# Delta rule: rows of decays put on all partitions by loads from memory, all sample states scaled on GpSimd during the input projection

## The reference

```python
g = -exp(a_log) * softplus(a_pre + dt_bias)          # log decay per token and head
gc = cumsum(g, within a chunk)
dmat = where(incl, exp(gc[:, None] - gc[None, :]), 0)
a_mat = strict lower part of (k * beta) k^T * dmat    # solved as (I + a_mat)^-1
qk = lower part of q k^T * dmat
q_dec, k_dec, g_last = q * exp(gc), k * exp(gc[last] - gc), exp(gc[last])
# chunk by chunk: v_new = u - w S ; o = q_dec S + qk v_new ; S = S g_last + k_dec^T v_new
```

## Time and profile before

| | |
|---|---|
| time before, median of 3 runs | 1590.81 us (1590.49 to 1592.78) |
| the profiled execution's own time | 1594.32 us |
| its span | 1592.6 us |
| busy: PE, DVE, ACT, POOL | 98%, 66%, 56%, 16% |
| granted PE clock and transfers, 98 to 104 us | 1.00, 176 GB/s |
| the same, 116 to 122 us | 1.00, 10 GB/s |
| the same, 128 to 134 us | 1.00, 0 GB/s |
| weight loads of 1 MB, median from issue to landing | 5.0 to 5.4 us for most, 8.3 for the delta rule's input weights |

### The profile page before, as it was taken

The page is one execution under the profiler, slowest core; times in us unless marked ns, Lnnn a source line. Parts: engine busy times, 40 slices in busy tenths (PEclk is TensorE's granted clock), DMA queues, the critical chain, the costliest instruction groups (busy, mean ns, idle before and its releaser), DMA issues.

```text
span 1592.6 us, 37769 instructions
## 1 busy us (share of the span) xinstructions
PE 1563.1 (98%) x16212; PEld 1481.5 (93%) x16212; DVE 1055.5 (66%) x1732; ACT 884.4 (56%) x1696; POOL 256.2 (16%) x328
## 2 busy tenths in 40 slices
PE   9999999999999999999999999999999999999997
PEld 7998799999997999999788888999999997999997
DVE  7965686755757877547793747776469837767643
ACT  6856656633645666434652546665358547566433
POOL 7105450000110200003003421100010035400000
PEclk9999999999999999999999999999999999999999
DMA  8941456565753665653635003665569512565550
GB/s 244 292 140 29 134 164 179 183 206 175 255 160 133 200 176 185 195 185 94 189 96 144 20 7 98 176 185 186 186 182 261 174 55 82 165 181 184 188 167 28
DMA packets 245529, 250.10 MB, mean 157 GB/s; under 512 B 16270, under 2 KB 239284, under 8 KB 245300
## 3 DMA queue, kind: packets, MB, share of 16 engines
q1 hardware_dynamic: 237204, 224.78, 46.3%
q0 software_dynamic: 8016, 22.86, 4.9%
q10 hardware_dynamic: 144, 0.05, 0.0%
HBM read 229.75 MB, written 18.32 MB: 156 GB/s over the span
## 4 chain that ended last, share of the span: by engine, by line
PE 92%; ACT 4%; DVE 3%; issue 1%; DMA 0%; SPq 0%; DVEq 0%
PE ps L844 88%; PE ps L848 4%; ACT vk L2053 1%; ACT tri L2053 1%; ACT acts L2053 1%; ACT st L2053 0%; DVE acts L2760 0%; ACT hn L2053 0%; DVE tri L2752 0%; DVE acts L2752 0%; DMA acts<-in_x_sample_dram 0%; ACT L2056 0%; PE ps L1796 0%; DVE st L2760 0%; DVE hn L2760 0%
## 5 line engine op out<-in xcount | busy, mean ns | idle before, releaser
L2752 DVE TENSOR_TENSOR w_mlp<-ring,w_mlp 128x1024 fp32r<-128x1024 f32 x256 | 311.7, 1224 | 119.9 <-ACT w_mlp L2053 113.9
L2053 ACT ACTIVATE w_mlp<-ring 128x1024 fp32r<-128x1024 f32 x256 | 269.4, 1054 | 208.2 <-PE ps L844 208.2
L844 PE MATMUL ps<-hn_split,w_mlp 128*128 128x264 f32 x3072 | 373.3, 284 | 0.0
L844 PE MATMUL ps<-h_split,w_mlp 128*128 128x264 f32 x3072 | 372.6, 283 | 0.0
L844 PEld LDWEIGHTS ps<-hn_split,w_mlp 128*128 128x128 f32 x3072 | 372.0, 188 | 0.3
L844 PEld LDWEIGHTS ps<-h_split,w_mlp 128*128 128x128 f32 x3072 | 371.6, 188 | 0.0
L2053 ACT ACTIVATE tri<-ps 128x264 f32<-128x264 f32 (+4 forms) x222 | 101.4, 463 | 181.2 <-PE ps L844 156.2
L844 PE MATMUL ps<-gdn_hi,w_gdn 128*128 128x264 f32 x896 | 165.8, 285 | 0.0
L844 PEld LDWEIGHTS ps<-gdn_hi,w_gdn 128*128 128x128 f32 x896 | 139.3, 188 | 0.9 <-issue 0.8
L844 PE MATMUL ps<-mixer_lo,w_gdn 128*128 128x264 f32 x448 | 126.9, 283 | 0.0
L2752 DVE TENSOR_TENSOR tri<-tri 128x264 f32<-128x264 f32 (+4 forms) x145 | 59.7, 413 | 101.3 <-ACT h_split L2053 100.6
(11 more groups left out here) (454 smaller groups left out, 2654.2 us busy)
## 6 DMA issues: line engine op xcount, KB each, us to landing
ring<-in_ffn_w_dram SPq DMA_DIRECT2D x128, 1024.0 KB, 5.4
ring<-in_gdn_w_in_dram SPq DMA_DIRECT2D x32, 1024.0 KB, 8.3
ring<-in_ml_w_in_dram SPq DMA_DIRECT2D x12, 1024.0 KB, 5.5
ring<-in_rw_w_rkv_dram SPq DMA_DIRECT2D x12, 1024.0 KB, 5.0
st<-in_state_gdn_S_dram POOLq DMA_DIRECT2D x2, 4096.0 KB, 22.4
ring<-in_gdn_w_out_dram SPq DMA_DIRECT2D x8, 1024.0 KB, 5.0
out_gdn_S_s_dram<-st SPq DMA_DIRECT2D x16, 512.0 KB, 6.8
st<-in_state_mlstm_C_dram POOLq DMA_DIRECT2D x1, 4096.0 KB, 20.5
```

The source lines that it names most:

```text
L844: return nc.tensor.matmul(out, lhsT, rhs, start=start, stop=stop)
L2053: return nc.scalar.activation(out, in_, f, bias=bias, scale=scale)
L2752: return nc.vector.tensor_tensor(out, in0, in1, op)
```

## The change

1. ACT, `gate_logs`: behind the logarithm it waits for DVE's `g_ok` and takes the exponential of the samples' 8x8 log decays (`eg_ev`). POOL puts it on a diagonal, PE multiplies it by ones in a new hook after u = 6 (`sample_decays`), and DVE copies the product to `E6[:, 5]` at n = 14.
2. POOL scales all eight heads of the sample states right behind that, during the projection. ACT's scaling is gone, and the outer products wait for no scaling.
3. The four `spread` calls and `spread_queries` are gone. After u = 13 PE makes one product of 16 rows and 256 columns. ACT copies it (log rows), takes its exponential and stores both in memory with five transfers from its own queue. POOL waits for them and issues three loads that repeat the rows: two of 64 partitions by 8 KB (into `AT6` and `QK6`), one of 128 partitions by 8 KB (into `QS`). DVE waits for all three before it adds `negC` to both matrices.
4. In `decay_exponents` five `ccol` products are left; POOL's two memsets now stand ahead of `rtx`. `statio` lies in another part of `acts`.

```diff
@@ PE
-                    for half in range(2):
-                        spread(0, 4 + half, half)
+                    b = 4
+                    pe.wait_ge(*last_read[b])
+                    mm(ps[b][0:2 * GH, 0:SEQ], selt[:, 0:2, :].rearrange("p a h -> p (a h)"), RG[:, 0:SEQ]).then_inc(row_mm, count.up(row_mm))
...
-                    for q in range(6):
+                    for n, q in enumerate((0, 1, 2, 3, 5)):
...
                 def query_exponents():
-                    for half in range(2):
-                        spread(4, 4 + half, half)
...
+                def sample_decays():
+                    pe.wait_ge(egd_ok, count.seen(egd_ok))
+                    b = 6
+                    pe.wait_ge(*last_read[b])
+                    mm(ps[b][:, 0:GH * NS], ones[0:GH, :], rows[0:GH, 1, 0:GH * NS]).then_inc(eg_mm, count.up(eg_mm))
...
-                fills = {(0, 0): sample_products, (0, 1): spread_queries, (1, 0): sample_outputs,
+                fills = {(0, 0): sample_products, (1, 0): sample_outputs,
@@ ACT, gate_logs
+                    ac.wait_ge(g_ok, count.seen(g_ok, 4 if j else 1))
+                    act(rows[0:GH, 1, SEQ:T], RG[0:GH, SEQ:T], ACT.Exp).then_inc(eg_ev, count.up(eg_ev))
@@ ACT, n == 27
+                        ac.wait_ge(row_mm, count.seen(row_mm))
+                        act(row_log, ps[4][0:2 * GH, 0:SEQ], ACT.Copy)
+                        act(row_exp, ps[4][0:2 * GH, 0:SEQ], ACT.Exp).then_inc(row_ev, count.up(row_ev))
+                        ac.wait_ge(row_ev, count.own(row_ev))
+                        for q in range(2):
+                            for g in range(2):
+                                at = q * GH + 4 * g
+                                ac.dma_start(exp_rows[j][g, q].rearrange("c h i -> h c i"),
+                                             rows[at:at + 4, 3, 0:SEQ].rearrange("h (c i) -> h c i", c=4)).then_inc(
+                                                 row_out, count.up(row_out, 16))
+                        ac.dma_start(query_rows[j], rows[0:GH, 4, 0:SEQ]).then_inc(row_out, count.up(row_out, 16))
...
-                    if n in (29, 30):
-                        ac.wait_ge(da_ok, count.seen(da_ok, 2))
-                        part = AT6 if n == 29 else QK6
-                        act(part, part, ACT.Exp).then_inc(dt_ok, count.up(dt_ok))
+                    if n == 30:
+                        for part in (AT6, QK6):
+                            ac.wait_ge(da_ok, count.seen(da_ok))
+                            act(part, part, ACT.Exp).then_inc(dt_ok, count.up(dt_ok))
@@ DVE
+                    if n == 14:
+                        dv.wait_ge(eg_mm, count.seen(eg_mm))
+                        copy(E6[:, 5], ps[6][:, 0:GH * NS]).then_inc(egs_ev, count.up(egs_ev))
...
-                exponents(QK6, 4, 0)
-                exponents(QK6, 5, 1)
+                dv.wait_ge(negc_ok, count.seen(negc_ok))
+                dv.wait_ge(spr_in, count.seen(spr_in, 48))
+                for part in (AT6, QK6):
+                    tt(part, part, negC, ALU.add).then_inc(da_ok, count.up(da_ok))
@@ POOL
+                for h in range(GH):
+                    s_ = sth[:, h]
+                    gp_.tensor_tensor(s_, s_, bc(E6[:, 5, h * NS:(h + 1) * NS], P, 2), ALU.mult).then_inc(
+                        st_sc, count.up(st_sc))
                 po.wait_ge(rt_ok, count.seen(rt_ok))
-                gp_.tensor_tensor(hs8(rtx), bc(RG[:, SEQ:T], GH, 1), bc(mh[:], NS, 2), ALU.mult).then_inc(rtx_ok, count.up(rtx_ok))
                 gp_.memset(statio, 0.0)
                 gp_.memset(vv, 0.0)
+                gp_.tensor_tensor(hs8(rtx), bc(RG[:, SEQ:T], GH, 1), bc(mh[:], NS, 2), ALU.mult).then_inc(rtx_ok, count.up(rtx_ok))
+                po.wait_ge(row_out, 80 * (j + 1))
+                for g, r in enumerate(halves):
+                    load(A(5).rearrange("p a b -> p (a b)")[r, 0:2 * D], bc(exp_rows[j][g].rearrange("s c h i -> (s c h i)"), HD, 0), spr_in)
+                load(QS.rearrange("p h t -> p (h t)"), bc(query_rows[j].rearrange("h t -> (h t)"), P, 0), spr_in)
```

More of the change, by code:

```diff
@@ L444, in hybrid_trunk @@
         ot_mm = oq_mm
-        qe_mm = rt_mm
         smp_mm = h_mm
         sp_mm = sw_mm
-        spread_mm = kk_mm
         ssq_ok = qs_ok
+        scan_ok = da_ok
+        row_mm = rt_mm
+        row_ev = rt_ok
+        egd_ok = qs_ok
+        qd_ok = st_sc
+        eg_mm = kk_mm
+        egs_ev = s_ok
         sums_mm = ct_mm
@@ L469, in hybrid_trunk @@
                     for i in range(2))
+        exp_rows = [nc.dram_tensor(f"exp_rows{n}", (2, 2, 4, 4, HD), F32, kind="Internal").ap() for n in range(2)]
+        query_rows = [nc.dram_tensor(f"query_rows{n}", (GH, SEQ), F32, kind="Internal").ap() for n in range(2)]
+        row_log, row_exp = rows[0:2 * GH, 3, 0:SEQ], rows[0:2 * GH, 4, 0:SEQ]
         QS = A(6).rearrange("p a b -> p (a b)")[:, 0:2 * D].rearrange("p (h t) -> p h t", h=GH)
-        statio = A(6).rearrange("p a b -> p (a b)")[:, 0:D].rearrange("p (h s n) -> p h s n", h=GH, s=NS)
+        statio = acts[:, 56:64, :].rearrange("p a b -> p (a b)")[:, 0:D].rearrange("p (h s n) -> p h s n", h=GH, s=NS)
         a7 = A(7).rearrange("p a b -> p (a b)")
@@ L1125, in sum_squares @@
                     last_read[b] = smp_ok, count.expect(smp_ok)
[L1127 to L1138, removed]
                 def gram(c, b):
@@ L1160, in decay_exponents @@
                             mm(ps[b][r, 16 * c:16 * c + 16].rearrange("p (q h) -> p q h", q=4), RG[:, c * HD:(c + 1) * HD],
[L1161 removed]
+                               selt[:, 1:5, 4 * g:4 * g + 4])
                     mm(ps[b][:, 64:96], ones[0:2 * GH, :], glm[0:2 * GH, :])
                     pe.wait_ge(rtx_ok, count.seen(rtx_ok))
[L1164 to L1165 removed]
+                    for n, q in enumerate((0, 1, 2, 3, 5)):
+                        last = mm(ps[b][:, P + n * 64:P + (n + 1) * 64], ccol[:, q:q + 1].broadcast_to([P, P]), rtx)
                     last.then_inc(cols_mm, count.up(cols_mm))
@@ L1179, in gdn @@
                 split_linear(gdn_hi, mixer_lo, 4 * D, evacuated, hnl_ok, banks=4, raw=gdn_raw[j], paired={(6, 5)[j]: lambda: norm(hn, KT - 2)},
-                             hooks={0: conv_states, 2.5: gates, 5: log_decays_to_columns, 7: cumulate_decays, 11: sum_squares, 13: decay_exponents,
+                             hooks={0: conv_states, 2.5: gates, 5: log_decays_to_columns, 6: sample_decays, 7: cumulate_decays, 11: sum_squares, 13: decay_exponents,
                                     14: query_exponents, 15: grams})
@@ L1199, in sample_products @@
                     last_read[b] = smp_ev, count.expect(smp_ev)
[L1201 to L1208, removed]
                 def token_major(c):
@@ L2341, in value_rows @@
                     last.then_inc(vkT_ev, count.up(vkT_ev))
[L2343 to L2347, removed]
                 def sample_norm():
@@ L3797, in masks @@
                     select(mh[:], [[-1, GH]], -32 * quad, 1, ALU.not_equal, 1.0)
-                for i, q in ((0, 0), (1, 3), (2, 6), (3, 6), (4, 1)):
+                for i, q in ((1, 0), (2, 3), (3, 6), (4, 6), (0, 1)):
                     last = gp_.tensor_tensor(selt[:, i, :], mh[:], ccol[:, q:q + 1].broadcast_to([P, GH]), ALU.mult)
                 done(last)
-                gp_.tensor_tensor(selt[:, 2, :], selt[:, 2, :], ident[:, GH:2 * GH], ALU.add).then_inc(consts, count.up(consts))
+                done(gp_.memset(ccol[0:32, 0:2], 0.0))
+                gp_.tensor_tensor(selt[:, 3, :], selt[:, 3, :], ident[:, GH:2 * GH], ALU.add).then_inc(consts, count.up(consts))
                 po.wait_ge(consts, count.own(consts))
```

52 lines of the change are left out of this document (23 added, 29 removed).

## The result

The changed kernel takes 1619.36 us (median of 4 runs, 1616.34 to 1621.05) against 1590.65 us for the one before (4 runs, 1589.84 to 1592.78): a ratio of 1.0175, interval 1.0157 to 1.0193. The forecast of 1589.4 us and its range of 1582.5 to 1596.0 were wrong. The change costs 28.7 us instead of giving 1.4.

The account below looks back on a forecast made before the run. TensorE was taken as the bound (92% of the span). Terms: -14.3 removed work, +0.4 `sample_decays`, +5.9 gate wait, +2.4 scaling, +4.2 row loads = -1.4 us, so 1589.4 us from 1590.8; range 1582.5 to 1596.

Parts of the forecast that it names:

- (d): Inversion: ScalarE loses four exponentials and 32 state scalings that hold up copies; -0.5 us per layer.
- What goes off PE: TensorE work removed in the delta rule, less what replaces it: -7.15 us per layer, -14.3 in all.
- (a): `decay_exponents`: key spread of 1.69 us replaced by a row product, one `ccol` product fewer; -1.3 us per layer.
- (b): `query_exponents`: the query spread, the same 32 matmuls, goes; -1.7 us per layer.
- (c): Inversion, between levels 0 and 1: `spread_queries` goes; -3.65 us per layer, only 2.5 if a PE gap opened.
- The gate wait: Gates: ScalarE waits for `g_ok`, so PE waits before tile 11: 3.35 us layer 0, 2.5 layer 3; +5.9.
- Turn-taking: Projection from tile 14: POOL's state scaling and VectorE delay each other; PE waits 1.2 us per layer (0 to 2.5), +2.4.
- The loads: Before the inversion: rows stored, then loaded, landing at 125.5; PE waits 2.1 us per layer (0.6 to 5.9), +4.2.
- The nearest price, 9.4: Row loads: one estimate for landing 2 MB, with 2.2 us fixed in the 512 KB row load; 8.5 was taken.
- cost no more: Row loads: the queries' rows, needed only from level 1 on, were said to add no cost.
- R2: Rival: row loads land late, at 129.3, and bound the inversion's start; sum +6.2, 1597.0 us; chance 0.2.
- the lower level: PE clock falling in a new wait, doubling matmul times behind it; listed as a sign of a wrong forecast.

Follow-up runs that it names:

- scaling half: Kernel before with only sample decays and state scaling on GpSimd during the projection, with the new gate wait; rows spread on TensorE as before: 1.0118, 1611.97 us.
- rows half: Kernel before with only the decay rows by a small product, stores and loads (also called the rows' kernel); scaling as before, no new gate wait: 1.0043, 1600.92 us.
- queries' kernel: Kernel before with only the queries' rows stored by ScalarE and loaded on SyncE's queue, instead of the spread between inversion levels 0 and 1: 0.9992.
- hardly any scaling: Changed kernel, but GpSimd's eight instructions scale 2 columns of each state instead of 128: 1.0106.
- no gate wait: Changed kernel, but ScalarE's exponential of the samples' decays reads its own rows, not VectorE's log decays, so the states' scaling numbers are wrong: 1.0103.
- split wait: Changed kernel, but VectorE waits only for its two loads and GpSimd alone for the third, on a semaphore of its own: 1.0122.
- products first: The mended change with TensorE's sample products ahead of level 0 of the inversion, in PSUM bank 2 instead of 6: 0.9963, 1586.39 us.
- mended change: Changed kernel with three repairs: VectorE waits for its two loads only, scaling six tiles later, ScalarE makes samples' decays from its own rows: 1.0004, 1591.88 us.
- mended change kept busy: The mended change with 8 products of constants, 128x256, results unread, in TensorE's wait before level 0: 1.0017.

## Why the prediction was wrong

The mechanisms were those named; four sizes were off: the removed query spread, the turn-taking, the landing of the rows, and the clock, which had no term at all. By halves: the sum charged 8.7 us to the scaling half (0.4 + 5.9 + 2.4), which alone measured 18.8, and -10.1 to the rows half (-14.3 + 4.2, with (d) counted here), which alone measured 6.8. So the rows half missed by 17 us, more than the scaling half by 10, though the scaling half makes most of the loss.

**What goes off PE.** (a) and (b) were right: from the row product to the end of the last gram it is 18.5 us (121.27 to 139.77) against 21.6, so 3.1 us against 3.0. (c) was mis-sized: 3.65 was read from PE alone. The sentence "Nothing else is late there" was wrong, as the queries' kernel shows (0.8 us of 3.65 kept). With POOL free, (c) gives 2.6 and (d) 0.2 (49.59 to 49.40), together 2.8 against the 4.15 charged.

**The gate wait.** Right in place and size: 3.10 and 2.90 us against 3.35 and 2.5. Wrong in what follows it, the clock: 1.9 us on tile 11 alone, and no term for it. Without the wait the kernel is 11.5 us faster, twice the term of 5.9.

**Turn-taking.** 1.2 us per layer (0 to 2.5) was charged; the waits are 4.1, and with the clock 11 us go in both layers together when there is hardly any scaling. The failed step is the delay of VectorE up to tile 18, put at 3 to 5 us. In layer 0 the longer instructions there sum to 7.3, of which 4.1 reach PE as waits: three weight parts take 1.04, 0.28 and 1.41 us more, where 0.42 a tile was charged; the sample convolution's copy and product take 1.69 and 1.59 more, about what the "two more such operations" were given; and the 16x32 product, which had no term, takes 1.43 instead of 0.18. A small instruction waits as long as a large one. The rule of the Trainium skill ("GPSIMD Engine Reference", Specifications) names also DVE instructions in a 2-port mode, which I had left out; the copy, with one SBUF input, isn't covered by the half that I quoted and waited all the same, though no run here shows its mode.

**The loads.** The landing was put at 125.5, at 129.3 in the worst case; less the 10.15 us by which the row product itself is late it was 130.8. Stores: 1.8 us by a row of a nearly empty POOL store, measured 5.0. Loads: 8.5 (7.0 to 12.3), measured 11.0. The nearest price, 9.4, took 2.2 us as fixed, which no row shows; a straight line through its own two rows (512 KB in 4.0, 4 MB in 22.4 us) gives 11.9 for 2 MB, an estimate that would have come close. All 2 MB stood behind one wait, though the prediction had itself seen that half of them is needed only at level 1; "cost no more" was wrong by 4.1 us a layer. The Trainium skill's fit ("DMA: Bandwidth & Descriptors", Anatomy of one DMA) gave 6.8 us for 2 MB; the trace disagrees with 11.0 for three loads that had the engines to themselves, and the moving alone took some 7.5 of it. R2 was the nearest rival and still too mild, since it left the other terms as they were.

**The clock.** It fell behind waits of 3.10, 2.61 and 7.53 us. Constants in the first and the last of these, in both layers, gave back 6.7 us. The prediction had the lower level as a sign of being wrong and no price for it.

By runs: no gate wait 11.5, hardly any scaling 11.0, split wait 8.4 us. Their sum of 30.9 is 3 us over the whole, and with the repaired forms of all three the change stands at 1.0004.

## What to carry to other kernels

A wait put on an engine that is the bound costs its length and often the clock behind it: look first for ready work to stand in it. A product that is taken off the bound engine is worth only what its neighbours can deliver earlier; read their timelines in the same stretch. GpSimd work beside VectorE is priced by how full VectorE is there: the same 18 us cost 8 us less, moved by six tiles.

## What the runs showed that was not expected

- A wait of 1.33 us at the row product was followed by the lower clock in one profile (0.50 from 113 to 116 us, layer 0 alone) and by none in another with the same instructions up to there. With the products first it was in both layers (0.50 from 118 to 120 and from 1282 to 1284 us), and in the rows' kernel once behind 0.54 us (0.50 from 114 to 116). So in these profiles the length of the wait doesn't tell by itself whether the clock falls. Executions of one kernel differ by as much as 9 us with it: of the ten of the mended change kept busy, the shortest (1591.02 us) had a mean granted clock of 0.997 and the longest (1600.33) 0.990.
- Filling a wait with useless matmuls made the changed kernel faster (1.0133 against 1.0175); in the mended kernel it gave nothing on the whole (1.0017 against 1.0004).
- Stores of 4 and 8 KB from ACT's queue took 5.0 us until the waiting engine went on, against 1.8 in the row I had used. What of it is the transfer, the way to memory or the weight load beside it was not tried: in every profile with these five stores such a load of 1 MB ran beside them. In the queries' kernel the one store of 8 KB, issued at 111.72, had no load beside it, and the DMA engines moved its bytes by 113.0; when it was complete no row shows.
